# A two-layer streaming encoder on one core: a new order at both ends of its expert layers

## The chip, the cores and the metric

The kernel runs on one core of a Trainium2 chip. The metric is device time in microseconds of one execution. Before the change the median of three runs is 1529.91 us (1525.41 to 1532.59).

## What is computed

576 tokens of width 1024 (512 of a new stream, 64 of a running one) pass two layers. Layer 0 mixes tokens with an RG-LRU and an HGRN2 branch, layer 1 with an S5 state space and a gated output. After each mixer comes a normalization of alpha*x + f(x), then a mixture of 16 experts, then another normalization. Cut to what matters here:

```python
def _moe(x, router_w, router_b, w_gate, w_up, w_down):
    ...
    y = jnp.zeros(xt.shape, F32)
    for e in range(N_EXPERTS):
        h = jax.nn.silu(xt @ w_gate[e]) * (xt @ w_up[e])
        y = y + combine[:, e:e + 1] * (h @ w_down[e]).astype(F32)
    return y.reshape(Bn, T, D).astype(x.dtype)

def _post_norm(x, f, g, b):
    s = ALPHA * x.astype(F32) + f.astype(F32)
    mu = jnp.mean(s, -1, keepdims=True)
    var = jnp.mean(jnp.square(s - mu), -1, keepdims=True)
    return ((s - mu) * lax.rsqrt(var + LN_EPS) * g.astype(F32) + b.astype(F32)).astype(x.dtype)
```

Each token goes to two of the 16 experts. `w_gate` and `w_up` of an expert are 1024 x 512, `w_down` is 512 x 1024, all float32.

## The kernel before

The five engines run programs of their own (PE, ACT, DVE, POOL and SP) that wait on semaphores. A float32 product is made of three passes (`mm3`, lines 2276 to 2278): each operand is split into a rounded part "hi" and a remainder "lo". ACT makes hi by a copy that rounds, DVE makes lo by a subtraction, and PE adds hi*lo, lo*hi and hi*hi.

The tokens are first scattered by POOL to a buffer `xg` in memory, 96 rows (`CAP`) for each expert. For expert `it` the steps are:

- SP loads the three weight matrices, 2 MB each, into `raw[0]` (gate), `raw[1]` (up) and `raw[2]` (down), one buffer for each kind (line 547). A load waits until DVE has made the remainder of the matrix before it in this buffer (semaphores `lo0`, `lo1`, `lo2`).
- ACT rounds `raw[q]` to `whi[q]` (line 607), DVE subtracts to `wlo[q]` (line 685). Rounding waits for the load (`ld0` to `ld2`) and until PE has finished with the `whi[q]` of the expert before (`p_g`, `p_u`, `p_d`).
- PE transposes the expert's rows (`xt`, line 754), ACT and DVE split them (`xet_hi` line 613, `xet_lo` line 689).
- PE makes the gate product, up(0,it), and the up product, up(1,it), of 24 matmuls each (line 765). ACT takes Silu of the first (line 620), DVE multiplies it by the second (`h`, line 695).
- PE transposes that (`ht`, line 773), ACT and DVE split it (`ht_hi` line 626, `ht_lo` line 699), and PE makes the down product, down(it), of 24 matmuls (line 786).
- ACT evicts it to `ysb` (`y_ev`, line 632), and POOL stores it to `yg` (line 584). There is one `ysb`: an eviction waits for the store before it (`y_st`).

The order of each engine is written out by hand in the functions `step` of `experts_act`, `experts_dve` and `experts_pe`. PE runs up(0,it), ht(it-1), up(1,it), xt(it+1), down(it-1). The last expert has code of its own: its down weights are loaded in two halves, and each half is rounded, subtracted and multiplied by itself. Behind the experts POOL loads scale and bias of the normalization (`lng`, `lnb`, line 275), waits for the last store, and gathers each token's two rows from `yg` (line 839). DVE adds them to the residual and normalizes (lines 858 to 308). In layer 0, ACT and DVE split the first two halves of S5's input matrix (lines 1133 and 1300) before that.

Behind the 16 experts each engine reads a step count that the router has computed, and branches: tokens that found no place among the 96 rows of an expert would get further rounds of 16 steps.

## Time and profile before

| | |
|---|---|
| median of three runs | 1529.91 us (1525.41 to 1532.59) |
| the profiled execution | 1527.47 us |
| its span, first to last instruction | 1525.5 us |
| mean granted clock of PE | 0.872 of full speed |
| PE, DVE, ACT, POOL busy | 82%, 67%, 46%, 13% of the span |
| moved by DMA | 301.79 MB, 198 GB/s over the span |
| chain that ended last | PE 40%, DVE 24%, DMA 20%, ACT 9%, issue 5% |

The two expert layers lie at about 374 to 717 us (with the gathers' start) and 1140 to 1480 us of the span. Busy shares are means over stages with different limits, so the stages are looked at one by one. An engine's idle time before an instruction is given with what ended it. A "load" lands when its semaphore is raised.

### The profile page before, as it was taken

The numbers are of one execution on the slowest core, as the hardware profiler recorded it, in microseconds if no ns is written. First come the engines' busy times: TensorE is split into PE (matmuls) and PEld (weight loads), VectorE is DVE, ScalarE is ACT, GpSimd is POOL, SyncE is SP. The second block draws the span as 40 slices with busy tenths as digits, with TensorE's granted clock in tenths as the row PEclk, the third lists the DMA queues.
The fourth block names the chain that finished last, engine by engine and source line by source line (L and its number), as shares of the span: only waits on it lengthen the run. The fifth ranks groups of instructions, "written<-read, shape, count | busy, mean of one in ns | idle before, by whom it ended". The sixth has DMA issues, their size and how long they took to land.

```text
span 1525.5 us, 17350 instructions
## 1 busy us (share of the span) xinstructions
PE 1248.8 (82%) x6836; PEld 999.0 (65%) x6836; DVE 1021.9 (67%) x1039; ACT 701.5 (46%) x623; POOL 193.9 (13%) x219
## 2 busy tenths in 40 slices
PE   6999998796789999995694363999967899999950
PEld 5898888576667766763473253977756677776730
DVE  5883666346368888885867997343463688888828
ACT  4632333003367777774124243631332677777720
POOL 2020000000200000002203961000003000000021
PEclk9998997795699999997795676999966999999985
DMA  9455000412789999987453007351026899999845
GB/s 274 183 61 112 31 35 4 124 82 110 255 299 375 379 369 382 384 335 247 103 93 60 0 7 58 115 191 56 1 110 232 318 356 384 381 383 377 347 146 154
DMA packets 79568, 301.79 MB, mean 198 GB/s; under 512 B 23189, under 2 KB 40945, under 8 KB 66897
## 3 DMA queue, kind: packets, MB, share of 16 engines
q1 hardware_dynamic: 63416, 246.07, 47.4%
q0 software_dynamic: 16096, 54.96, 11.6%
q8 instruction: 38, 0.62, 0.2%
q14 instruction: 18, 0.14, 0.0%
HBM read 265.01 MB, written 33.64 MB: 196 GB/s over the span
## 4 chain that ended last, share of the span: by engine, by line
PE 40%; DVE 24%; DMA 20%; ACT 9%; issue 5%; SPq 1%; POOL 0%; POOLq 0%; ACTq 0%; DVEq 0%
PE ps L2276 9%; PE ps L2277 9%; PE ps L2278 9%; DVE wlo L685 7%; DMA raw<-in_moe_w_down 7%; DMA raw<-in_moe_w_gate 7%; ACT whi L607 6%; PE ps L746 3%; DMA u_d<-ub 2%; PE ps L1682 2%; PE ps L373 2%; DMA raw<-in_moe_w_up 1%; DMA raw<-in_w_in_ab 1%; DVE s_jtmp L1484 1%; PE ps L2386 1%
## 5 line engine op out<-in xcount | busy, mean ns | idle before, releaser
L685 DVE TENSOR_TENSOR wlo<-raw,whi 128x4096 fp32r<-128x4096 f32 x92 | 407.1, 4425 | 129.8 <-ACT whi L607 129.6
L607 ACT ACTIVATE whi<-raw 128x4096 fp32r<-128x4096 f32 x92 | 333.7, 3627 | 117.3 <-DMA raw<-in_moe_w_down 77.4
L2276 PE MATMUL ps<-whi,xet_lo 128*96 128x512 f32 x512 | 208.9, 408 | 28.4 <-ACT hx L620 24.3
L2277 PE MATMUL ps<-wlo,xet_hi 128*96 128x512 f32 x512 | 205.8, 402 | 0.0
L2278 PE MATMUL ps<-whi,xet_hi 128*96 128x512 f32 x512 | 205.8, 402 | 0.0
L2276 PEld LDWEIGHTS ps<-whi,xet_lo 128*96 128x96 f32 x512 | 86.3, 169 | 69.2 <-issue 35.7
L2276 PE MATMUL ps<-ft_hi,wlo 128*128 128x288 f32 x384 | 120.0, 312 | 5.1 <-DVE wlo L2023 3.6
L2277 PE MATMUL ps<-ft_lo,whi 128*128 128x288 f32 x384 | 116.9, 304 | 0.1
L2278 PE MATMUL ps<-ft_hi,whi 128*128 128x288 f32 x384 | 116.6, 304 | 0.0
L2276 PE MATMUL ps<-whi,ht_lo 128*96 128x512 f32 x256 | 104.1, 407 | 10.4 <-DVE ht_lo L699 8.7
L2278 PEld LDWEIGHTS ps<-whi,xet_hi 128*96 128x96 f32 x512 | 85.0, 166 | 37.1
L2277 PEld LDWEIGHTS ps<-wlo,xet_hi 128*96 128x96 f32 x512 | 85.2, 166 | 33.5 <-issue 0.5
L2276 PE MATMUL ps<-whi,ft_lo 128*120 128x512 f32 (+1 forms) x240 | 96.6, 403 | 11.8 <-DVE ft_lo L1308 6.1
L2278 PE MATMUL ps<-whi,ht_hi 128*96 128x512 f32 x256 | 102.2, 399 | 0.0
L2277 PE MATMUL ps<-wlo,ht_hi 128*96 128x512 f32 x256 | 102.1, 399 | 0.0
L2277 PE MATMUL ps<-wlo,ft_hi 128*120 128x512 f32 (+1 forms) x240 | 95.8, 399 | 0.0
L2278 PE MATMUL ps<-whi,ft_hi 128*120 128x512 f32 (+1 forms) x240 | 95.5, 398 | 0.0
L2276 PEld LDWEIGHTS ps<-ft_hi,wlo 128*128 128x128 f32 x384 | 76.2, 198 | 7.1 <-issue 6.3
L2277 PEld LDWEIGHTS ps<-ft_lo,whi 128*128 128x128 f32 x384 | 76.0, 198 | 0.5 <-issue 0.2
L2278 PEld LDWEIGHTS ps<-ft_hi,whi 128*128 128x128 f32 x384 | 75.6, 197 | 0.0
L584 POOL DMA_DIRECT2D yg<-ysb x32 | 16.2, 505 | 404.7 <-ACT ysb L632 404.7
L613 ACT ACTIVATE xet_hi<-ps 128x768 fp32r<-128x768 f32 x32 | 25.9, 809 | 83.5 <-PE ps L746 50.7
(449 smaller groups left out, 2234.9 us busy)
## 6 DMA issues: line engine op xcount, KB each, us to landing
raw<-in_moe_w_gate SPq DMA_DIRECT2D x32, 2048.0 KB, 9.9
raw<-in_moe_w_up SPq DMA_DIRECT2D x32, 2048.0 KB, 9.9
raw<-in_moe_w_down SPq DMA_DIRECT2D x30, 2048.0 KB, 10.2
yg<-ysb POOLq DMA_DIRECT2D x32, 384.0 KB, 6.0
xe<-xg POOLq DMA_DIRECT2D x30, 384.0 KB, 8.7
raw<-in_w_in_ab SPq DMA_DIRECT2D x16, 512.0 KB, 7.5
raw<-in_w_out_s SPq DMA_DIRECT2D x4, 2048.0 KB, 8.2
xg<-zeros POOLq DMA_DIRECT2D x4, 1536.0 KB, 14.5
```

The lines of the kernel that those rows point to most:

```text
L373: ins = te.matmul(ps[0:n, 6, E * i:E * i + E], x1t[:, k, 0:n], rw[:, k, :], start=(k == 0), stop=(k == KT - 1))
L584: pool.dma_start(rows, ysb[0:CAP, :]).then_inc(s("y_st" + L), 16)
L607: sa.activation(whi[q][:], raw[q][:], ACT.Copy).then_inc(s(f"hi{q}" + L), 1)
L613: sa.activation(xe_rows(xet_hi), xe_banks, ACT.Copy).then_inc(s("xth" + L), 1)
L685: v.tensor_tensor(wlo[q][:], raw[q][:], whi[q][:].bitcast(F32), ALU.subtract).then_inc(s(f"lo{q}" + L), 1)
L746: ins = te.matmul(ps[:, 4 + k // 4, P * (k % 4):P * (k % 4) + CAP], xtok[0:n, i, k:D:KT], onehot[0:n, i, :], start=(i == 0), stop=(i == NT ...
L1484: ins = tt(jtmp[:, k, 0:n], src, poles[lv][:, k, :, pairs].rearrange("p (x r) a -> p x r a", x=1).to_broadcast([P, n, 2, QP]), M)
L1682: ins = te.matmul(out, spad[(i // 2) % 2][:, ri, pair % QP, b, :], ox[:, ri, 1:CL + 1, pair, :], start=False, stop=(ri == 1))
L2276: te.matmul(out, l_lo, r_hi, start=first, stop=False)
L2277: te.matmul(out, l_hi, r_lo, start=False, stop=False)
L2278: return te.matmul(out, l_hi, r_hi, start=False, stop=last)
L2386: return te.matmul(out, vtok[rows, q // 2, :], sc[rows, q // 2, :], start=(q == 0), stop=True)
```

## The change

The start of a layer:

- ACT rounds and DVE subtracts the down weights of expert 0 before the tokens have arrived (`hi(2, 0)`, `lo(2, 0)`).
- In ACT's `step(it)`, Silu of expert `it` follows the split of the hidden rows of `it-1` and stands ahead of the rounding of the next gate weights. Before, it opened the step after.
- In DVE's `step(it)`, `h(it)` stands between the remainders of the next gate weights and the next tokens. Before, it opened the step after.

The end of a layer:

- The last down weights are loaded whole, into `raw[0]`, as soon as the remainder of the last gate weights is made, and split into `whi[0]` and `wlo[0]`.
- PE puts the transposes of the last hidden rows between the halves of down(14). Their split goes to `xet_hi` and `xet_lo`, and the last down product goes to the PSUM banks 0 and 1.
- In layer 0, the split of the first half of S5's input matrix (`s5_hi`, `s5_lo`, through `raw[1]`, now) stands ahead of the last eviction on ACT. The second half goes through `raw[0]`.
- POOL issues the loads of scale and bias ahead of the last store. The bias has a place of its own (`lnb_f`, over `ht_hi` and `ht_lo`), so its load waits for down(14).
- The wait for the last store moves into `gather`, behind the reading of the step count and the branch.

The core of the diff:

```diff
         def ln_gains_pool(pool, tag):
...
+            pool.dma_start(lng[:], a[f"ln_{ln}_g"][l:l + 1, :].to_broadcast([P, D])).then_inc(s("ln_gains"), 16)
+            if ln == "ffn":
+                pool.wait_ge(s(f"p_d_{l}"), E - 1)
+            pool.dma_start(lnb[:] if ln == "mix" else lnb_f[:], a[f"ln_{ln}_b"][l:l + 1, :].to_broadcast([P, D])
+                           ).then_inc(s("ln_gains"), 16)
...
         def experts_sp(sp_, l):
...
-            sp_.wait_ge(s("lo2" + L), E - 1)
-            for h_, name in enumerate(("ld2", "ld0")):
-                sp_.dma_start(raw[2][:, half * h_:half * h_ + half].rearrange("p (k n) -> p k n", k=2),
-                              w3[2][:, E - 1, 2 * h_:2 * h_ + 2]).then_inc(s(name + L), 16)
+            sp_.wait_ge(s("lo0" + L), E)
+            sp_.dma_start(raw[0][:].rearrange("p (k n) -> p k n", k=4), w3[2][:, E - 1]).then_inc(s("ld0" + L), 16)
...
         def experts_pool(pool, l):
...
-            for it in range(E - 3, E):
+            for it in range(E - 3, E - 1):
                 store_y(it)
+            pool.wait_ge(s("p_xt" + L), E)
+            ln_gains_pool(pool, f"ffn{l}")
+            store_y(E - 1)
...
-        def experts_act(act, l):
+        def experts_act(act, l, early=None):
...
-            def step(it, prev=True, prev2=True, nxt=True):
-                if prev:
-                    silu(it - 1)
+            def step(it, prev=True, prev2=True, nxt=True, down=True):
+                if prev and down:
                     hi(2, it - 1, "p_d")
                 if prev2:
                     y_ev(it - 2)
                 if prev:
                     ht_hi_(it - 1)
+                silu(it)
                 if nxt:
                     hi(0, it + 1, "p_g")
                     xt_hi(it + 1)
                     hi(1, it + 1, "p_u")

             hi(1, 0, "")
+            hi(2, 0, "")
             xt_hi(0)
             step(0, prev=False, prev2=False)
-            step(1, prev2=False)
+            step(1, prev2=False, down=False)
...
+            act.wait_ge(s("ld0" + L), 16 * E + 16)
+            act.wait_ge(s("p_g" + L), E)
+            for h_ in range(2):
                 half = slice(CHUNK // 2 * h_, CHUNK // 2 * h_ + CHUNK // 2)
...
+                sa.activation(whi[0][:, half], raw[0][:, half], ACT.Copy).then_inc(s("hi0" + L), 1)
+            act.wait_ge(s("p_ht" + L), E)
+            act.wait_ge(s("p_u" + L), E)
+            sa.activation(xet_hi[:, 0:4, 0:CAP], h_bank, ACT.Copy).then_inc(s("hth" + L), 1)
+            y_ev(E - 2)
+            if early:
+                early()
+            act.wait_ge(s("p_d" + L), E)
+            act.wait_ge(s("y_st" + L), 16 * E - 16)
+            sa.activation(ysb[0:CAP, :].rearrange("p (a c) -> p a c", a=2), ps[0:CAP, 0:2, :],
+                          ACT.Copy).then_inc(s("y_ev" + L), 1)
...
         def experts_dve(dve, l, early=None):
...
-            def step(it, prev=True, nxt=True):
+            def step(it, prev=True, nxt=True, down=True):
+                if prev and down:
+                    lo(2, it - 1)
                 if prev:
-                    h(it - 1)
-                    lo(2, it - 1)
                     ht_lo_(it - 1)
                 if nxt:
                     lo(0, it + 1)
+                    h(it)
                     xt_lo(it + 1)
                     lo(1, it + 1)
...
         def experts_pe(pe, mm3, l):
...
-            step(E - 1, nxt=False)
-            ht(E - 1)
+            up(0, E - 1, "p_g")
+            ht(E - 2)
+            up(1, E - 1, "p_u")
+            down(E - 2, between=E - 1)
...
         def combine_pool(pool, l):
             L = f"_{l}"
-            ln_gains_pool(pool, f"ffn{l}")
-            pool.wait_ge(s("y_st" + L), 16 * E)

             def gather(rows):
+                pool.wait_ge(s("y_st" + L), 16 * E)
                 for i, (t0, n) in enumerate(TILES):
...
         def s5_sp(sp_):
...
-            sp_.wait_ge(s("lo0_0"), E)
+            sp_.wait_ge(s("lo1_0"), E)
             load(0)
-            sp_.wait_ge(s("lo1_0"), E)
+            sp_.wait_ge(s("lo0_0"), E + 2)
             load(1)
...
-            experts_act(act, 0)
+            experts_act(act, 0, lambda: s5_hi(act, 0))
...
-            experts_dve(dve, 0)
+            experts_dve(dve, 0, lambda: s5_lo(dve, 0))
```

How the change moves instructions is shown at three places. Each row is an instruction with its line, what it writes and reads, and the semaphores it waits for. `whi_51` and `raw_49` are the buffers 0, `whi_52` and `raw_50` the buffers 1, `whi_164` (`whi_165` in the changed kernel) the buffer 2; `_0` at a semaphore's end is layer 0. The changed kernel's line numbers are higher by 1 to some 24.

ACT at the start of layer 0's experts, before:

```order
L607 ACTIVATE whi_52<-raw_50 128x4096 [waits ld1_0]
L613 ACTIVATE xet_hi<-ps 128x8x96 [waits p_xt_0]
L607 ACTIVATE whi_51<-raw_49 128x4096 [waits p_g_0,ld0_0]
L613 ACTIVATE xet_hi<-ps 128x8x96 [waits p_u_0,p_xt_0]
L607 ACTIVATE whi_52<-raw_50 128x4096 [waits p_u_0,ld1_0]
L620 ACT_TABLE_LOAD
L620 ACTIVATE hx<-ps 96x512 [waits p_g_0]
L607 ACTIVATE whi_164<-raw_163 128x4096 [waits ld2_0]
```

And in the changed kernel:

```order
L611 ACTIVATE whi_52<-raw_50 128x4096 [waits ld1_0]
L611 ACTIVATE whi_165<-raw_164 128x4096 [waits ld2_0]
L617 ACTIVATE xet_hi<-ps 128x8x96 [waits p_xt_0]
L624 ACT_TABLE_LOAD
L624 ACTIVATE hx<-ps 96x512 [waits p_g_0]
L611 ACTIVATE whi_51<-raw_49 128x4096 [waits p_g_0,ld0_0]
L617 ACTIVATE xet_hi<-ps 128x8x96 [waits p_u_0,p_xt_0]
L611 ACTIVATE whi_52<-raw_50 128x4096 [waits p_u_0,ld1_0]
```

The Silu (`hx`) with its table load has moved ahead of the rounding of the next gate weights, and the rounding of the first down weights ahead of the first tokens.

ACT at the end of layer 0's experts, before, from the split of expert 14's hidden rows:

```order
L626 ACTIVATE ht_hi<-ps 128x4x96 [waits p_d_0,p_ht_0]
L620 ACTIVATE hx<-ps 96x512 [waits p_ht_0,p_g_0]
L664 ACTIVATE whi_164<-raw_163 128x2048 [waits ld2_0,p_d_0]
L632 ACTIVATE ysb<-ps 96x1024 [waits y_st_0,p_d_0]
L626 ACTIVATE ht_hi<-ps 128x4x96 [waits p_d_0,p_ht_0]
L664 ACTIVATE whi_164<-raw_163 128x2048 [waits ld0_0]
L632 ACTIVATE ysb<-ps 96x1024 [waits y_st_0,p_d_0]
```

And in the changed kernel:

```order
L630 ACTIVATE ht_hi<-ps 128x4x96 [waits p_d_0,p_ht_0]
L624 ACTIVATE hx<-ps 96x512 [waits p_ht_0,p_g_0]
L668 ACTIVATE whi_51<-raw_49 128x2048 [waits p_g_0,ld0_0]
L668 ACTIVATE whi_51<-raw_49 128x2048
L671 ACTIVATE xet_hi<-ps 128x4x96 [waits p_u_0,p_ht_0]
L636 ACTIVATE ysb<-ps 96x1024 [waits y_st_0,p_d_0]
L1153 ACTIVATE whi_52<-raw_50 128x2048 [waits w_landed1]
L1153 ACTIVATE whi_52<-raw_50 128x2048
L677 ACTIVATE ysb<-ps 96x1024 [waits y_st_0,p_d_0]
```

The last down weights are rounded into buffer 0, waiting for the last gate product (`p_g`) and no longer for down(14) (`p_d`), and S5's first matrix half stands between the last two evictions.

POOL from the last stores to the first gather of layer 0, before, with the rows of the branch that is not taken left out of both pieces:

```order
L584 DMA yg<-ysb 96x1024 [waits y_ev_0] x3
L522 TENSOR_LOAD nstep [waits routed]
...
L275 DMA lng<-in_ln_ffn_g 128x1024
L275 DMA lnb<-in_ln_ffn_b 128x1024
L522 TENSOR_LOAD nstep [waits routed,y_st_0]
L522 ISA x2
L844 COMPARE_AND_BRANCH
L839 DMA ygat_167<-yg,slot 120x1024
```

And in the changed kernel:

```order
L585 DMA yg<-ysb 96x1024 [waits y_ev_0] x2
L276 DMA lng<-in_ln_ffn_g 128x1024 [waits p_xt_0]
L279 DMA lnb_f<-in_ln_ffn_b 128x1024 [waits p_d_0]
L585 DMA yg<-ysb 96x1024 [waits y_ev_0]
...
L527 TENSOR_LOAD nstep [waits routed]
L527 ISA x2
L863 COMPARE_AND_BRANCH
L858 DMA ygat_168<-yg,slot 120x1024 [waits y_st_0]
```

The two loads have moved ahead of the third store, and the wait for the store (`y_st`) from the second reading of the step count to the first gather.

## Rows read from the trace of the kernel before

**Rows 1.** Windows: us, then busy us (instructions) by engine, granted clock, DMA share, GB/s
```profile
412.00:470.00 58.00, 49.42 (x211) 35.07 (x212) 41.57 (x18) 42.28 (x22) 2.02 (x4) 0.91 0.85 310
470.00:510.00 40.00, 40.00 (x191) 29.05 (x190) 33.24 (x13) 28.55 (x17) 2.21 (x5) 1.00 1.00 392
...
677.00:700.00 23.00, 21.64 (x98) 15.15 (x96) 14.22 (x7) 11.09 (x7) 0.51 (x1) 1.00 0.61 229
```
**Rows 2.** Timeline of SP's queue: start us, us, engine, line, op; gate weights, experts 5, 15
```profile
475.45 0.33 SPq L547 DMA_DIRECT2D raw<-in_moe_w_gate  x1
...
660.81 0.33 SPq L547 DMA_DIRECT2D raw<-in_moe_w_gate  x1
```
**Rows 3.** Timeline of ACT, start of layer 0's experts; in brackets idle time before, what ended it
```profile
360.88 1.28 ACT L355 ACT_TABLE_LOAD   x1
364.67 0.27 ACT L355 ACTIVATE r_p<-r_w 120x80 f32<-120x80 f32 x1 [2.51 <-DVE r_w L423]
...
404.09 3.62 ACT L607 ACTIVATE whi<-raw 128x4096 fp32r<-128x4096 f32 x1 [9.49 <-PE ps L2278]
...
414.71 1.28 ACT L620 ACT_TABLE_LOAD   x1
416.00 0.59 ACT L620 ACTIVATE hx<-ps 96x512 f32<-96x512 f32 x1
```
**Rows 4.** Timeline of DVE, start of layer 0's experts
```profile
407.75 4.43 DVE L685 TENSOR_TENSOR wlo<-raw,whi 128x4096 fp32r<-128x4096 f32 x1 [12.16 <-ACT whi L607]
412.09 0.95 DVE L689 TENSOR_TENSOR xet_lo<-ps,xet_hi 128x768 fp32r<-128x768 f32 x1
```
**Rows 5.** Timeline of PE, first matmuls of the gate products of experts 1 and 2
```profile
416.74 0.71 PE L2276 MATMUL ps<-whi,xet_lo 128*96 128x512 f32 x1 [6.40 <-ACT hx L620]
...
441.00 0.44 PE L2276 MATMUL ps<-whi,xet_lo 128*96 128x512 f32 x1 [3.84 <-ACT hx L620]
```
**Rows 6.** DMA issues: the whole span's gate loads; then, 640 to 775, halves and stores
```profile
raw<-in_moe_w_gate SPq DMA_DIRECT2D x32, 2048.0 KB, 9.9
...
raw<-in_moe_w_down SPq DMA_DIRECT2D x2, 1024.0 KB, 6.5
yg<-ysb POOLq DMA_DIRECT2D x5, 384.0 KB, 5.7
```
**Rows 7.** Timeline of PE, last expert's matmuls: 1st and 13th of layer 0, 1st of layer 1
```profile
703.25 0.74 PE L2276 MATMUL ps<-whi,ht_lo 128*96 128x512 f32 x1 [4.35 <-DVE ht_lo L699]
...
708.47 0.39 PE L2276 MATMUL ps<-whi,ht_lo 128*96 128x512 f32 x1
...
1466.59 0.74 PE L2276 MATMUL ps<-whi,ht_lo 128*96 128x512 f32 x1 [4.35 <-DVE ht_lo L699]
```
**Rows 8.** Timeline of ACT, end of layer 0's experts
```profile
682.40 3.63 ACT L607 ACTIVATE whi<-raw 128x4096 fp32r<-128x4096 f32 x1 [1.33 <-DMA raw<-in_moe_w_down]
...
698.50 1.91 ACT L664 ACTIVATE whi<-raw 128x2048 fp32r<-128x2048 f32 x1 [10.00 <-PE ps L2278]
...
711.41 1.02 ACT L632 ACTIVATE ysb<-ps 96x1024 f32<-96x1024 f32 x1 [7.93 <-PE ps L2278]
```
**Rows 9.** Timeline of DVE, end of layer 0's experts
```profile
675.40 4.43 DVE L685 TENSOR_TENSOR wlo<-raw,whi 128x4096 fp32r<-128x4096 f32 x1 [0.26 <-ACT whi L607]
...
686.07 4.43 DVE L685 TENSOR_TENSOR wlo<-raw,whi 128x4096 fp32r<-128x4096 f32 x1 [0.43 <-ACT whi L607]
...
693.08 0.68 DVE L695 TENSOR_TENSOR hx<-hx,ps 96x512 f32<-96x512 f32 x1 [2.11 <-PE ps L2278]
```
**Rows 10.** Chain that ended last: start us, us, what; the last store of each layer
```profile
712.73 3.26 DMA yg<-ysb
...
1475.06 3.21 DMA yg<-ysb
```
**Rows 11.** Timeline of POOL, the first gather of each layer
```profile
717.59 2.10 POOL L839 DMA_INDIRECT ygat<-yg,slot  x1 [2.48 <-issue]
...
1480.21 1.02 POOL L839 DMA_INDIRECT ygat<-yg,slot  x1 [2.78 <-issue]
```

More of the change, by code:

```diff
@@ L532, in experts_sp, with load @@
                   a["moe_w_down"][l].rearrange("e (p k) n -> p e k n", p=P)]
-            half = CHUNK // 2
-            def load(q, e, it, further=0):
+            def load(q, e, it, done=0):
                 if isinstance(it, int) and it == 0:
@@ L711, in experts_dve @@
             lo(1, 0)
+            lo(2, 0)
             xt_lo(0)
             step(0, prev=False)
-            with dve.Fori(1, E - 1) as it:
+            step(1, down=False)
+            with dve.Fori(2, E - 1) as it:
                 step(it)
             step(E - 1, nxt=False)
-            h(E - 1)
             for h_ in range(2):
-                dve.wait_ge(s("hi2" + L), E + h_)
+                dve.wait_ge(s("hi0" + L), E + 1 + h_)
                 half = slice(CHUNK // 2 * h_, CHUNK // 2 * h_ + CHUNK // 2)
-                v.tensor_tensor(wlo[2][:, half], raw[2][:, half], whi[2][:, half].bitcast(F32),
-                                ALU.subtract).then_inc(s("lo2" + L), 1)
+                v.tensor_tensor(wlo[0][:, half], raw[0][:, half], whi[0][:, half].bitcast(F32),
+                                ALU.subtract).then_inc(s("lo0" + L), 1)
                 if h_ == 0:
-                    ht_lo_(E - 1)
+                    h(E - 1)
+            dve.wait_ge(s("hth" + L), E)
+            v.tensor_tensor(xet_lo[:, 0:4, 0:CAP], h_bank, xet_hi[:, 0:4, 0:CAP].bitcast(F32), ALU.subtract).then_inc(s("htl" + L), 1)
+            if early:
+                early()
             steps = step_count(dve, l)
@@ L755, in xt, with up @@
                 ins.then_inc(s("p_xt" + L), 1)
-            def up(q, it, done):
-                pe.wait_ge(s(f"lo{q}" + L), it + 1)
+            def up(q, it, done, more=0):
+                pe.wait_ge(s(f"lo{q}" + L), it + (1 + more))
                 pe.wait_ge(s("xtl" + L), it + 1)
@@ L774, in ht, with down @@
                 ins.then_inc(s("p_ht" + L), 1)
-            def down(it, further=0):
-                pe.wait_ge(s("lo2" + L), it + (1 + further))
+            def down(it, more=0, between=None):
+                pe.wait_ge(s("lo2" + L), it + (1 + more))
                 pe.wait_ge(s("htl" + L), it + 1)
@@ L787, in down @@
                                   k == 0, k == 3)
+                    if half == 0 and between is not None:
+                        ht(between)
                 ins.then_inc(s("p_d" + L), 1)
@@ L1291, in s5_act, with s5_lo @@
             x1t_copy(act, 1, NT - 2)
+        def s5_lo(dve, c):
+            tt, k = nc.vector.tensor_tensor, split_slot[c]
+            for h_ in range(2):
+                dve.wait_ge(s("hi_done"), s5_split(c, h_))
+                tt(wlo_s5[k][:, half_of(h_)], raw[raw_slot[c]][:, half_of(h_)], whi_s5[k][:, half_of(h_)].bitcast(F32),
+                   ALU.subtract).then_inc(s("lo_done"), 1)
         def s5_dve(dve, link, split_lo):
```

86 lines of the change are left out of this document (37 added, 49 removed).

## The prediction

> **What bounds the kernel now.** I read the windows first, then the waits at both ends of the expert layers, then the queues that feed them. In the windows [rows 1] the reader is to see three kinds of stretch. From 470 to 510 PE is busy for all of its 40.00 us, the clock is at 1.00 of full speed (2.4 GHz) and the DMA share is 1.00 at 392 GB/s: the loop over the experts is full on two resources at once. From 412 to 470, at the layer's start, PE has 49.42 busy of 58 us (8.6 idle), the clock averages 0.91 and DMA 0.85. From 677 to 700, at its end, DMA has dropped to 0.61. The SP queue [rows 2] gives the loop's pace: gate weights for expert 5 are requested at 475.45, for expert 15 at 660.81, so 18.54 us per expert. What a better order can win lies at the ends; inside, the same bytes must still move.
>
> **Start of a layer.** PE idles 6.40 us before up(0,1) and 3.84 us before up(0,2), both times ended by ACT's Silu [rows 5]. Silu of expert 0 had its product long before: ACT takes the rounding of gate(1) at 404.09 as soon as PE's gate product of expert 0 is done, then more work, then the table load at 414.71, and only at 416.00 the Silu [rows 3]. In the new order Silu stands ahead of that rounding. Its table load (1.28 us) can run while ACT waits for PE: an earlier table load at 360.88 ran ahead of an activation that then still waited 2.51 us for its input [rows 3]; ACT idled 9.49 us before 404.09, so I cost it at nothing. If that cover is gone, the price is 1.28 per layer.
> So Silu(0) runs 404.1 to 404.7, rounding gate(1) takes 3.62 to 408.3, DVE's remainder 4.43 to 412.8 (before: 407.75 + 4.43 = 412.2, so 0.6 later) [rows 3, 4]. Then DVE does h(0), now ahead of the token remainder: 0.68 [rows 9], then 0.95 [rows 4], to 414.5. PE starts up(0,1) there, not at 416.74: 2.2 us gained. At up(0,2) the Silu stood behind the scaling of the residual on ACT; now it is ahead of it, and the operands of expert 2 come from gate(2)'s load, whose request moved by +0.6 only. The down weights of expert 0 are rounded before the tokens arrive, while ACT and DVE wait (9.49 us and more), at no cost, and their buffer is then free for the next load at once, where before DVE freed it only after expert 1's other remainders. I count the whole 3.84 as gone: 6.0 together. With no stop, PE also keeps more of its clock; of the 0.09 that the mean granted clock lacks over 58 us (5.2 us of full-speed time, part of it in idle time) I take 0.8. **Start: 6.8 per layer.** Above, PE's idle time (8.6) and the DMA's free share (0.15 x 58 = 8.7) bound it at 8.6. Below, the bound is 0, if the loop gives it back.
>
> **The loop.** Silu (0.59) now precedes the rounding of the next gate weights on ACT, and h (0.68) precedes the token remainder and the up remainder on DVE. A load lands 9.9 us after its request in the loop, while the two halves of a down load at the layer's end land in 6.5 [rows 6]. The difference, some 3 us, is time spent queued behind other loads (an estimate from these two rows). A request that comes 0.6 to 1.3 us later only queues less. I cost the loop at 0.
>
> **End of a layer, layer 0.** PE waits 4.35 us for the last expert's hidden remainder and restarts at half speed: 12 matmuls take 703.25 to 708.47, 5.22 us, and the other 12 to the eviction at 711.41, 2.94 us [rows 7, 8]. The cause is that ACT may round the last down weights only when PE has released their buffer (the idle time of 10.00 before 698.50 ended by PE) [rows 8]. In the new order these weights land in buffer 0. They are requested after the gate remainder of expert 15, 675.40 + 4.43 = 679.8 [rows 9]. Queued behind the load that lands at 682.40 [rows 8], 2.10 MB at 392 GB/s take 5.35, so they land at 687.8. Two halves of 1.91 on ACT go to 691.6 [rows 8]. DVE finishes the down remainder of expert 14 at 686.07 + 4.43 = 690.5, then a half (2.2), h at 693.08 + 0.68 = 693.8 (up(1,15) ends it, as before), the other half to 696.0 [rows 9]. PE needs h in the middle of down(14), at about 695.5, and the halves when down(14) and the transposes end: 703.25 - 4.35 = 698.9. All are early by 1.7 us or more, so the 4.35 vanish and the restart too: 5.22 - 2.94 = 2.3. PE is done 6.65 earlier, at 704.8.
> Three things are added in front of the last eviction. ACT's two halves for S5's first matrix half (3.8) begin after the eviction of expert 14, at 700.0, and end at 703.8, before 704.8; if the matrix half landed after 701 it would hold the eviction. The eviction now also really waits for the store of expert 14: evicted 698.9 to 700.0, requested at 700.2, landing 5.7 later in this stretch [rows 6], 705.9. That costs 1.1. On POOL the two loads of scale and bias (1 MB) now stand ahead of the last store; their waits end with down(14), and POOL issues them before 702, so the instruction order costs nothing.
> The gathers now pass their branch first and then wait for the store. Before, the store lands at 712.73 + 3.26 = 715.99 [rows 10] and the first gather goes at 717.59 [rows 11]: 1.6 between them, filled by the reading of the step count and the branch; I take all of it. The Trainium skill (Advanced Engine Details and Errata, Control Flow Timing) puts a branch at 51 ns and a compare with branch at 108 ns. By that page alone little would be won by moving the wait, and the sum would stand at about 1502.5 instead. No row here prices the branch without the load of the step count.
> The DVE work on S5's matrix (before it ended shortly ahead of the first gathered rows) is earlier by about as much, so the gathers stay the last to arrive. **End of layer 0: 6.65 - 1.1 + 1.6 = 7.1.**
>
> **End of layer 1.** The last store is issued 8.47 after PE's restart (1466.59 to 1475.06), against 9.48 in layer 0, so the cold part is 1.0 shorter and PE's gain is 5.65. No S5 load competes; a store lands in 3.21 [rows 10], so the eviction does not wait for it. The gather follows its store's landing (1478.27) at 1480.21 [rows 11]: 1.9. **7.6.** The final normalizations follow unchanged.
>
> **Sum.** 2 x 6.8 + 7.1 + 7.6 = 28.3. The profiled execution took 1527.5 (span 1525.5 and 2.0 around it): **1499**. The median of the runs shown, 1529.9, stands 2.4 above that execution.
>
> **Rivals.**
> *The loop gives the start back (0.15).* If the loop is paced by something that the earlier start does not move, the first experts only queue longer, and 14.7 remains: 1512.8. For it: DMA is already at 1.00 by 470. Against: the bytes that did not move at 0.85 were lost time, and the total is the same.
> *The shared DMA engines delay the stores (0.07).* The scale and bias, 1 MB, move while the stores of experts 14 and 15 go out; at 392 GB/s they take 2.7. If each layer's last stores wait that long, layer 0 loses 2.7, layer 1 2.7 less the 1.1 of slack there: 1503.5. For it: a store's 5.7 near S5's loads against 3.21 alone [rows 6, 10]. Against: it is likely that most of that megabyte has moved by 705. The Trainium skill (DMA: Bandwidth & Descriptors, Issuing engines are not separate DMA queues) says that all issuers share the same 16 DMA engines, which speaks against putting these loads ahead of the store. The rows agree that neighbours stretch a store; no run here yet shows it for these loads.
> *The loop gets longer (0.05).* If not the DMA's rate but the ring of each buffer (load, round, remainder, next request) sets 18.54 us, then Silu and h lie on it: 0.59 + 0.68 = 1.27 in each of 13 turns in 2 layers, 33.0; the start's gain is lost too: 1527.5 - 14.7 + 33.0 = 1545.8, slower. It decides once a load's queueing time is under 1.27; the rows give some 3 [rows 6].
> *Nothing is won at either end (0.03)*, because a late landing holds ACT in front of the last eviction and the loop takes the start: 1527.
>
> **How the numbers follow.** The forecast has 0.70. The low end is both starts at 8.6 and no wait for the store, 1494.5, less some 3.5 for the spread of the runs (1525.4 to 1532.6): 1491. The high end holds the first rival and part of the second on top: 1516. About 0.5% (7.6 us) is what a measurement of this kernel can tell from no change. The forecast, the first two rivals and no more are faster by that: 0.91, of which I give 0.90; same 0.05, slower 0.05.
>
> **What would show it.** Right: PE's waits for Silu gone from both starts; the same 18.5 us between gate requests, shifted by 6 to 7; no PE idle time and a granted clock of 1.00 up to the last matmul of a layer; the first gather right behind its store's landing, 13 to 15 us earlier. Wrong: a pace above 19 us per expert; a wait of PE for h inside down(14); ACT waiting for S5's matrix ahead of the last eviction; the last eviction late behind a store.

## The result, and the profile after

The changed kernel takes **1507.02 us** (median of four runs, 1503.28 to 1510.12) where the kernel before takes 1531.06 (four runs, 1525.41 to 1532.59): a ratio of **0.984, interval 0.981 to 0.986**. The forecast was 1499 us, faster, with a range of 1491 to 1516. Two more comparisons, made beside the experiments below, gave 0.980 (0.978 to 0.982) and 0.984 (0.982 to 0.987).

The page of the changed kernel: span, busy time, and the chain that ended last.

```profile
span 1502.1 us, 17364 instructions
PE 1242.7 (83%) x6836; PEld 995.0 (66%) x6836; DVE 1019.8 (68%) x1039; ACT 701.2 (47%) x623; POOL 199.3 (13%) x219
PE 57%; DVE 20%; DMA 12%; ACT 5%; issue 4%; SPq 2%; POOL 0%; DVEq 0%; ACTq 0%; POOLq 0%
```

The span is 23.4 us shorter. PE has grown from 40% to 57% of the chain, DMA has gone from 20% to 12%. The windows, to be laid beside [rows 1] (the whole program lies 3.4 us later here when the experts of layer 0 begin):

```profile
412.00:470.00 58.00, 54.12 (x250) 38.92 (x249) 43.65 (x18) 41.37 (x23) 3.07 (x6) 0.97 0.89 340
470.00:510.00 40.00, 39.87 (x185) 28.28 (x184) 33.55 (x16) 29.79 (x15) 2.03 (x4) 1.00 1.00 384
...
677.00:700.00 23.00, 22.71 (x104) 16.20 (x103) 17.14 (x9) 14.24 (x10) 2.11 (x4) 1.00 0.81 296
```

At the start PE is busy for 54.1 of 58 us, not 49.4, and the granted clock is 0.97, not 0.91. At the end the DMA share is 0.81, not 0.61. The loop between is as full as it was, and its pace is 18.6 us per expert, against 18.54 in [rows 2] (gate weights of experts 5 and 15):

```profile
471.71 0.33 SPq L551 DMA_DIRECT2D raw<-in_moe_w_gate  x1
...
657.73 0.33 SPq L551 DMA_DIRECT2D raw<-in_moe_w_gate  x1
```

**The start.** ACT's timeline, beside [rows 3], and PE's, beside [rows 5]:

```profile
398.14 1.28 ACT L624 ACT_TABLE_LOAD   x1
407.44 0.60 ACT L624 ACTIVATE hx<-ps 96x512 f32<-96x512 f32 x1 [8.01 <-PE ps L2302]
407.93 3.62 ACT L611 ACTIVATE whi<-raw 128x4096 fp32r<-128x4096 f32 x1
```
```profile
417.57 0.45 PE L2300 MATMUL ps<-whi,xet_lo 128*96 128x512 f32 x1 [3.82 <-issue]
```

The table load runs while ACT waits for PE, so its cover held. Silu runs as soon as PE's product is done, and the rounding follows it at once. The wait of 6.40 us before up(0,1) is down to 3.82 us, and the one of 3.84 us before up(0,2) is gone: PE has no other wait up to 475.

**The end of layer 0.** ACT from the eviction of expert 14, and POOL up to the first gather:

```profile
695.25 1.02 ACT L636 ACTIVATE ysb<-ps 96x1024 f32<-96x1024 f32 x1 [2.26 <-PE ps L2302]
696.18 3.70 ACT L1153 ACTIVATE whi<-raw 128x2048 fp32r<-128x2048 f32 x2
702.63 1.02 ACT L677 ACTIVATE ysb<-ps 96x1024 f32<-96x1024 f32 x1 [2.74 <-DMA yg<-ysb]
```
```profile
696.57 0.51 POOL L585 DMA_DIRECT2D yg<-ysb  x1 [11.70 <-ACT ysb L636]
697.07 0.57 POOL L276 DMA_DIRECT2D lng<-in_ln_ffn_g  x1
697.62 0.56 POOL L279 DMA_DIRECT2D lnb_f<-in_ln_ffn_b  x1
703.94 0.53 POOL L585 DMA_DIRECT2D yg<-ysb  x1 [5.77 <-ACT ysb L677]
707.70 1.02 POOL L858 DMA_INDIRECT ygat<-yg,slot  x1 [3.23 <-DMA yg<-ysb]
```

PE has no idle time left between up(0,15), from 677.64 on, and the last matmul; the 4.35 us of [rows 7] and the restart are gone. The last eviction waits for the store of expert 14, as forecast. The first gather follows the landing of the last store (requested at 703.94, landed 3.46 later) by 0.3 us, where it was 1.6.

**By stretches.** The table cuts each profile at the same five events: POOL's first scatter of a layer, SP's requests for the gate weights of experts 5 and 15, DVE's first addition of gathered rows, and the end. Every number is the difference of two rows' start times, in us. "Ahead" is all before the first scatter, code that no kernel here changes. The stretch between the layers' experts (418.5 to 419.6) and the one behind the last addition (37.2 to 37.3) are alike in all kernels and left out.

| kernel | ahead | start 0 | loop 0 | end 0 | start 1 | loop 1 | end 1 | span |
|---|---|---|---|---|---|---|---|---|
| before | 379.5 | 96.0 | 185.4 | 65.7 | 95.3 | 184.4 | 63.6 | 1525.5 |
| changed, 1st | 382.9 | 88.8 | 186.0 | 57.9 | 89.2 | 185.3 | 56.3 | 1502.1 |
| changed, 2nd | 382.9 | 89.8 | 182.2 | 59.0 | 89.3 | 185.6 | 57.2 | 1502.4 |
| changed, 3rd | 385.6 | 89.5 | 188.5 | 59.8 | 87.7 | 187.3 | 57.5 | 1512.3 |
| start only | 387.8 | 88.8 | 185.6 | 65.0 | 89.4 | 186.2 | 64.2 | 1523.8 |
| order only | 386.0 | 87.7 | 182.2 | 65.0 | 88.8 | 187.9 | 63.2 | 1516.5 |
| end only | 381.0 | 96.2 | 186.9 | 60.0 | 95.6 | 187.0 | 57.0 | 1520.1 |
| wait back | 382.2 | 89.5 | 185.1 | 60.5 | 89.5 | 186.9 | 57.6 | 1507.4 |
| loads behind | 386.2 | 89.6 | 190.9 | 61.3 | 89.4 | 188.7 | 58.0 | 1520.2 |
| S5 behind | 385.8 | 89.4 | 186.4 | 59.4 | 88.0 | 186.1 | 56.9 | 1508.7 |
| S5 held | 388.8 | 88.5 | 186.3 | 71.2 | 87.4 | 184.1 | 57.3 | 1520.4 |
| two moves | 382.6 | 87.4 | 188.8 | 59.6 | 88.3 | 186.5 | 57.1 | 1506.9 |
| three moves | 382.1 | 87.7 | 185.1 | 58.2 | 86.4 | 185.7 | 56.9 | 1498.7 |
| loop twice | 387.7 | 90.3 | 190.4 | 60.7 | 90.3 | 187.3 | 57.9 | 1521.3 |

In the first pair (before, and changed 1st) the change is worth 7.2 and 6.1 us at the starts and 7.7 and 7.3 at the ends, the loops give back 0.7 and 0.9, and unchanged code ahead took 3.4 more: 23.4. Over the three profiles of the changed kernel the means are 89.4 and 88.7 at the starts and 58.9 and 57.0 at the ends, against 96.1 and 95.5 (two kernels with the old start) and 65.2 and 63.7 (three with the old end): 6.7 + 6.7 + 6.3 + 6.7 = **26.4 us**, which is also what the mean of the three ratios gives (1 - 0.983, times 1531: 26).

### The profile page after: what moved, and what is told of

Read it like the earlier page. It is cut to its first block, busy times and chain, and to the rows that moved or that the text cites. A ratio compares the mean times of both kernels' runs of the same rounds, so it can differ in the third digit from the quotient of the medians.

```text
span 1502.1 us, 17364 instructions
## 1 busy us (share of the span) xinstructions
PE 1242.7 (83%) x6836; PEld 995.0 (66%) x6836; DVE 1019.8 (68%) x1039; ACT 701.2 (47%) x623; POOL 199.3 (13%) x219
## 4 chain that ended last, share of the span: by engine, by line
PE 57%; DVE 20%; DMA 12%; ACT 5%; issue 4%; SPq 2%; POOL 0%; DVEq 0%; ACTq 0%; POOLq 0%
PE ps L2300 15%; PE ps L2302 14%; PE ps L2301 14%; DMA raw<-in_moe_w_down 7%; DVE wlo L695 4%; ACT whi L611 3%; PE ps L762 3%; DMA u_d<-ub 2%; PE ps L1706 2%; PE ps L378 2%; DVE s_jtmp L1508 1%; DMA raw<-in_w_in_ab 1%; PE ps L2410 1%; DVE s_wt L1465 1%; PE ps L1704 1%
## 5 line engine op out<-in xcount | busy, mean ns | idle before, releaser
L2300 PE MATMUL ps<-whi,xet_lo 128*96 128x512 f32 x528 | 213.5, 404 | 18.1 <-issue 13.6
L2302 PE MATMUL ps<-whi,xet_hi 128*96 128x512 f32 x528 | 210.6, 399 | 0.0
L2301 PE MATMUL ps<-wlo,xet_hi 128*96 128x512 f32 x528 | 210.3, 398 | 0.0
L2300 PE MATMUL ps<-whi,ht_lo 128*96 128x512 f32 x240 | 96.1, 401 | 1.6 <-DVE wlo L695 1.5
L2302 PE MATMUL ps<-whi,ft_hi 128*120 128x512 f32 (+1 forms) x240 | 95.6, 398 | 0.0
L2302 PE MATMUL ps<-whi,ht_hi 128*96 128x512 f32 x240 | 94.6, 394 | 0.0
L2301 PE MATMUL ps<-wlo,ht_hi 128*96 128x512 f32 x240 | 94.5, 394 | 0.0
L340 POOL DMA_INDIRECT xg<-xtok,slot x20 | 30.2, 1510 | 249.2 <-issue 248.9
```

What stands on the lines that cost most here:

```text
L340: pool.indirect_dma_start(out=xg, out_offset=bass.IndirectOffsetOnAxis(ap=slot[0:n, k, i:i + 1], axis=0), in_=xtok[0:n, i, :], in_offset=N ...
L2300: te.matmul(out, l_lo, r_hi, start=first, stop=False)
L2301: te.matmul(out, l_hi, r_lo, start=False, stop=False)
L2302: return te.matmul(out, l_hi, r_hi, start=False, stop=last)
```

## The experiments

Each kernel is compared with the kernel before on the same chip.

### Start only, order only, end only

The start alone is the kernel before with the start's lines of the diff; the order alone leaves out the early split of the down weights; the end alone is the changed kernel with the old lines there.

```diff
 start only, on ACT (DVE likewise with lo, h):
+            hi(2, 0, "")
...
-                if prev:
-                    silu(it - 1)
...
+                silu(it)
                 if nxt:
 order only, against the start only:
-            hi(2, 0, "")
-            lo(2, 0)
```

> The kernel before with the new order at the start of a layer alone. Theory of the forecast (the start's waits for Silu go, the loop keeps its pace of 18.5 us per expert): in the pair of profiles the start was worth 7.2 us in layer 0 and 6.1 in layer 1, so 13.3 us less than the kernel before, a ratio of 0.991; the request for the gate weights of expert 5 comes 6 to 7 us earlier, counted from the router's last stage, and PE's wait of 4.35 us before the last expert's down product stays. Rival, the loop gives the start back: ratio 1.000, the request for expert 15 not earlier at all. Rival, Silu and h lengthen the loop: about 33 us more in the loops, ratio 1.01.

> The changed kernel with the old order at the start of a layer: the end alone. Theory: the last gate request to the first gather is shorter by 6.8 us in layer 0 and 7.0 in layer 1, and the rows then arrive another 0.9 earlier, 14 to 15 us in all, a ratio of 0.990 to the kernel before; PE's waits of 6.40 and 3.84 us at the start are back, PE has no wait from up(0,15) to the last matmul. Rival (nothing is won at the end, since the last eviction waits for a landing): ratio 0.998 or more. If both parts are independent, this ratio times that of the start alone is the changed kernel's 0.984.

> The start of a layer alone, and of it only the places of Silu and h; the down weights of expert 0 are split where they were before. Theory of the forecast (both waits of PE are ended by a Silu that stands too late, so the order alone removes them): the stretch from the first scatter to the request for the gate weights of expert 5 takes 88.8 to 90.5 us in layer 0 (before 95.99, with the whole start 88.75) and 89.2 to 91 in layer 1 (before 95.29, with the whole start 89.44). Rival (the early split frees a buffer early, and the earlier load is what gains): 92 to 95 us in both.

Measured: start only 1522.56 us, ratio 0.993 (0.990 to 0.996); end only 1520.91, ratio 0.991 (0.988 to 0.994); order only 1520.66, ratio 0.991 (0.988 to 0.994). PE's first waits at the start, in the end-only kernel (two rows, columns as in [rows 5]) and in the order-only kernel (one row):

```profile
418.48 0.71 PE L2297 MATMUL ps<-whi,xet_lo 128*96 128x512 f32 x1 [6.40 <-ACT hx L624]
442.80 0.44 PE L2297 MATMUL ps<-whi,xet_lo 128*96 128x512 f32 x1 [3.84 <-ACT hx L624]
```
```profile
420.05 0.71 PE L2276 MATMUL ps<-whi,xet_lo 128*96 128x512 f32 x1 [3.82 <-issue]
```

And the start-only kernel has the old wait at the last expert:

```profile
704.66 0.74 PE L2279 MATMUL ps<-whi,ht_lo 128*96 128x512 f32 x1 [4.35 <-DVE ht_lo L699]
```

The two halves of the change are independent: each moves its own stretch and no other, and 0.993 times 0.991 is 0.984. The loop does not give the start back. And the order of Silu and h is all of the start's gain: with the down weights split in their old place the starts are 87.7 and 88.8 us, no longer than with the whole (88.8 and 89.4). The early split is worth nothing. Silu on ACT and h on DVE were moved together; what each is worth alone is not shown.

### Three parts of the end

POOL's wait for the last store ahead of the step count again ("wait back"); the loads of scale and bias behind the last store ("loads behind"); S5's first split behind the last eviction ("S5 behind").

```diff
 wait back, in combine_pool:
+            pool.wait_ge(s("y_st" + L), 16 * E)
             def gather(rows):
-                pool.wait_ge(s("y_st" + L), 16 * E)
 loads behind, in experts_pool:
+            store_y(E - 1)
             pool.wait_ge(s("p_xt" + L), E)
             ln_gains_pool(pool, f"ffn{l}")
-            store_y(E - 1)
 S5 behind:
-            experts_act(act, 0, lambda: s5_hi(act, 0))
+            experts_act(act, 0)
...
+            hi(0)
             hi(1)
```

> The changed kernel with POOL's wait for the last store ahead of the second reading of the step count, as before. Theory: reading the step count and the branch come back between landing and gather, where the kernel before had 1.6 us (layer 0) and 1.9 (layer 1) and the changed kernel has 0.3 and 0.66: the first gather comes 1.3 us later in each layer, 2.6 us more than the changed kernel. Rival, by the Trainium skill's 51 ns for a branch: under 0.3 us in both layers together. The distance from landing to gather in the trace tells them apart, the total is near what the runs can tell.

> The changed kernel with the loads of scale and bias behind the last store, as before. Rival of the forecast (these 1 MB share the DMA engines with the stores of experts 14 and 15 and delay them): the store of expert 14 lands in 3.3 to 4.5 us instead of 5.8, the last eviction of layer 0 comes up to 1.9 us earlier, layer 1's last store lands in 3.2 instead of 3.86; 2 to 3 us less than the changed kernel. Theory of the forecast (the 5.8 is S5's load of 2 MB, the loads of scale and bias matter little): landing of the store of expert 14 between 5.3 and 5.9, last eviction within 0.5 us of the changed kernel's, total within 1 us of it.

> The changed kernel with the split of S5's first matrix half behind the last eviction again, on ACT and DVE. Theory of the forecast (the gathered rows are the last to arrive, this split only fills idle time): the first row block is added (DVE) as long after the request for the gate weights of expert 15 as in the changed kernel, 57.9 to 59.0 us, and S5 is not longer; total unchanged. Rival, the early split is a part of the gain: DVE's four remainders of 2.2 us each then end about 716 us into the span, after the rows; 1 to 3 us more in this stretch.

**Wait back**: 1512.68 us, ratio 0.987 (0.984 to 0.991). POOL's last store and first gather of each layer:

```profile
703.21 0.53 POOL L585 DMA_DIRECT2D yg<-ysb  x1 [5.72 <-ACT ysb L677]
708.10 2.09 POOL L858 DMA_INDIRECT ygat<-yg,slot  x1 [4.36 <-issue]
...
1456.51 0.53 POOL L585 DMA_DIRECT2D yg<-ysb  x1 [3.88 <-ACT ysb L677]
1462.32 1.02 POOL L858 DMA_INDIRECT ygat<-yg,slot  x1 [5.29 <-issue]
```

From store to gather are 4.89 and 5.81 us; in the three profiles of the changed kernel 3.5 to 3.8 and 4.5 to 5.0. Part of this is the store itself. Its time to landing stands in the chain that ended last (start us, us), in this kernel and then in the changed one:

```profile
703.21 3.29 DMA yg<-ysb
...
1456.51 3.89 DMA yg<-ysb
```
```profile
703.94 3.46 DMA yg<-ysb
...
1452.72 3.86 DMA yg<-ysb
```

From landing to gather are 1.60 and 1.92 us here, as in the kernel before, and 0.30 and 0.66 in the changed kernel. So reading the step count and branching cost 1.3 us in each layer where they stand behind the landing. The total is later than the changed kernel's, by no more than the comparisons differ.

**Loads behind**: 1517.72 us, ratio 0.988 (0.985 to 0.992). In layer 0, against the rival, the store of expert 14 did not land sooner: the last eviction (ACT) waited 4.05 us for it, where it waited 2.53 to 3.80 in the three profiles of the changed kernel.

```profile
703.67 1.02 ACT L636 ACTIVATE ysb<-ps 96x1024 f32<-96x1024 f32 x1 [2.26 <-PE ps L2302]
...
712.34 1.02 ACT L677 ACTIVATE ysb<-ps 96x1024 f32<-96x1024 f32 x1 [4.05 <-DMA yg<-ysb]
```

But that wait goes with another load. The earlier the 2 MB of S5's second half are requested ahead of this store, the closer the last two evictions start: 4.09 us ahead 7.16 apart, 3.45 ahead 7.38, 3.40 ahead 8.44 (the three profiles of the changed kernel), 3.00 ahead 8.67 (here, requested at 701.98 and 704.98), 2.64 ahead 9.03 (end only). So layer 0 cannot tell what scale and bias do to that store. In layer 1, where no such load competes, the last store landed in 3.21 us, as the rival had it, and in 3.86 to 4.29 with the loads in front of it.

The first gather came as soon behind the store as in the changed kernel (3.76 and 4.04 us), but its rows took longer to arrive: 10.55 and 9.83 us from the first gather to the first addition, against 7.9 to 8.7 and 7.6 to 8.2. The same 1 MB now runs beside the gathers. End 0 is 61.3 us against the three profiles' 58.9, end 1 is 58.0 against 57.0. That the rows come later is clear. That the earlier place of these loads is a gain, of one to two us, is likely and not shown: this is one profile, and two other kernels with the changed end have nearly as much in layer 0 (end only 60.0, loop twice 60.7). The forecast had only the danger.

**S5 behind**: 1512.60 us, ratio 0.985 (0.981 to 0.988), beside 0.984 for the changed kernel in that comparison. End 0 is 59.4, inside the changed kernel's 57.9 to 59.8. DVE's split and its first addition:

```profile
711.08 8.90 DVE L1321 TENSOR_TENSOR wlo<-raw,whi 128x2048 fp32r<-128x2048 f32 x4 [12.96 <-ACT whi L1153]
720.96 1.28 DVE L877 SCALAR_TENSOR_TENSOR xtok<-ygat,gate,xtok 120x1024 f32<-120x1024 f32 x1 [0.98 <-DMA ygat<-yg,slot]
```

Even with all four remainders in a row DVE is done 0.98 us before the rows. The early split of S5's half is worth nothing here; it leaves DVE more idle time (5.63 us before 715.65 in the changed kernel).

### The last eviction's wait

"Two moves": the last eviction gets a buffer of its own, and in the first step alone the rounding of gate(1) and the token remainder go ahead of Silu and h. "S5 held": the changed kernel with the load of S5's second half behind the last store. "Three moves": two moves, and that load through `raw[2]`, early.

```diff
 two moves:
+        ysb_last = at("ysb_last", [P, D], FT_AT)
-            act.wait_ge(s("y_st" + L), 16 * E - 16)
-            sa.activation(ysb[0:CAP, :]...
+            sa.activation(ysb_last[0:CAP, :]...
 S5 held:
-            sp_.wait_ge(s("lo0_0"), E + 2)
+            sp_.wait_ge(s("y_st_0"), 16 * E)
             load(1)
 three moves:
-            sp_.wait_ge(s("lo0_0"), E + 2)
+            sp_.wait_ge(s("lo2_0"), E - 1)
             load(1)
```

> The changed kernel with two more moves. The last eviction goes to a buffer of its own (over the down weights, which are then done with), so it does not wait for the store of expert 14; in the first step alone, the rounding of gate(1) stands ahead of Silu(0) and the remainder of the tokens ahead of h(0). Theory: in layer 0 the last store follows the one before it after 5.5 us as in layer 1, not 7.37: 1.9 us less; the start is shorter by Silu and h, 0.5 + 0.68 us, in each layer: 87.6 and 88.0 us; 4.2 us less than the changed kernel in all. Rival (the wait for the store is only replaced by a later landing of the last store, and the start by another wait): no difference in either stretch.

> The changed kernel with the load of S5's second matrix half (2 MB) held until the last store of layer 0 has landed. Theory (this load is the neighbour that stretches the last two stores; what the DMA engines move first costs the other): the store of expert 14 lands in 3.3 to 4.5 us instead of 5.9, the last store is requested 5.5 to 6 us behind it instead of 7.37 and 7.16; the 2 MB then meet the gathers, rows come 2 to 5 us later than the landing says (from first gather to first addition 10 to 13 us instead of 8 to 8.7). Rival (the neighbours that matter are scale and bias): landing still 5.5 to 5.9.

> The version with two more moves, and a third: the second half of S5's matrix is loaded through the buffer of the down weights, which is free some 6 us earlier, while the DMA engines are idle (the places of gathered rows are exchanged so that the first go elsewhere). Theory: that load has then landed ahead of the last two stores; layer 0's last store is requested 5.5 us behind the one before it and lands in 3.3 to 3.6, against 11.1 us for both in the changed kernel and 11.65 in the version with two moves: 9.0 to 9.4; with the starts (87.4 and 88.3 us) some 4 us less than the changed kernel. Rival: scale and bias alone stretch the last store, 10.5 to 11.5 us for both, and no more is gained than at the starts, some 2 us.

> The changed kernel once more, beside the version with two more moves on the same chip. Its ratio to the kernel before should lie at 0.984 as in the first comparison, and its stretches within 1 us of those of its first profile (start 88.8 and 89.2, last store 7.37 behind the one before it in layer 0).

> The changed kernel a third time, beside these on the same chip: ratio between the 0.980 and 0.984 of the two comparisons so far.

**Two moves**: 1506.60 us, ratio 0.979 (0.977 to 0.982), beside 1506.02 and 0.980 for the changed kernel. ACT's last eviction, then POOL's last store and first gather:

```profile
701.84 1.02 ACT L681 ACTIVATE ysb_last<-ps 96x1024 f32<-96x1024 f32 x1 [0.98 <-PE ps L2309]
```
```profile
703.15 0.52 POOL L587 DMA_DIRECT2D yg<-ysb_last  x1 [4.00 <-ACT ysb_last L681]
709.20 2.22 POOL L865 DMA_INDIRECT ygat<-yg,slot  x1 [5.53 <-DMA yg<-ysb_last]
```

The eviction now waits only for PE, and the last store is requested 5.60 us behind the one before it, not 7.37. But it lands later: the gather goes 6.05 us behind it, not 3.76. The two together are 11.65, against 11.13, 10.63 and 11.93 in the three profiles of the changed kernel. On the store the rival was right: the wait moved from the eviction to the landing. At the start PE's wait before up(0,1) is shorter in layer 0, 3.09 us and not 3.82:

```profile
416.76 0.44 PE L2307 MATMUL ps<-whi,xet_lo 128*96 128x512 f32 x1 [3.09 <-DVE wlo L699]
```

The starts are 87.4 and 88.3 us. Among the kernels that have the changed kernel's start and loop, the first is shorter than any (88.5 to 89.8) and the second is not (87.4 to 89.5).

**S5 held**: 1521.91 us, ratio 0.989 (0.986 to 0.993). ACT's last two evictions and its next rounding:

```profile
701.15 1.02 ACT L636 ACTIVATE ysb<-ps 96x1024 f32<-96x1024 f32 x1 [2.26 <-PE ps L2302]
...
706.63 1.02 ACT L677 ACTIVATE ysb<-ps 96x1024 f32<-96x1024 f32 x1 [0.86 <-PE ps L2302]
728.44 3.71 ACT L1153 ACTIVATE whi<-raw 128x2048 fp32r<-128x2048 f32 x2 [20.79 <-DMA raw<-in_w_in_s]
```

With the 2 MB out of the way the store of expert 14 lands in time and the eviction waits for PE alone: S5's load is the neighbour that stretches that store. The price was far above what I expected: beside the gathers the load took some 16 us (requested behind the landing at about 712), DVE stands in line behind it, and end 0 grows to 71.2. DVE adds the first rows right behind that split, so when they arrived cannot be seen.

**Three moves**: 1508.06 us, ratio 0.982 (0.979 to 0.984), beside 1514.03 and 0.984 (0.982 to 0.987) for the changed kernel. The last store is requested 5.48 us behind the one before and the gather follows 4.43 later, 9.91 together: less than in the changed kernel, between what was expected (9.0 to 9.4) and its rival (10.5 to 11.5). But the rows then take 9.84 us, and end 0 is 58.2. Four orders of the same bytes (changed, two moves, three moves, S5 behind) all reach the first addition 57.9 to 59.8 us after the last gate request. The starts are 87.7 and 86.4 against 89.5 and 87.7. The medians favour this version by 6 us, but the intervals overlap: that it beats the changed kernel is not shown.

### The loop

Silu (ACT, shown) and the token remainder (DVE, likewise) are executed twice in each turn of the loop.

```diff
                 if twice:
+                    sa.activation(hx[0:CAP, :], ps[0:CAP, 0, :], ACT.Silu)...
                 sa.activation(hx[0:CAP, :], ps[0:CAP, 0, :], ACT.Silu)...
```

> The changed kernel with Silu executed twice on ACT (0.6 us more) and the remainder of the token rows twice on DVE (0.95 us more) in each of the 13 turns of the loop; the second result is the same as the first. Theory (the ring of load, rounding, remainder and next request has slack, a later request only queues less): the ten experts from the request for expert 5 to that for expert 15 take 185 to 187 us, as in the changed kernel (186.0 and 185.3). Rival, the ring sets the pace: 0.6 + 0.95 for each expert, 201 us per loop and 40 us in all.

Measured: 1528.69 us, ratio 0.997 (0.995 to 0.999), beside 1506.02 and 0.980 for the changed kernel: 22.7 us more, of 40 added. The profile is that of the lowest of its ten runs (1523.08) and shows only some 6 us in the two loops (190.4 + 187.3 against means of 185.6 + 186.0). Windows in the loop of layer 0, of the changed kernel and of this one (columns as in [rows 1]):

```profile
480.00:660.00 180.00, 176.00 (x815) 125.14 (x814) 147.76 (x60) 130.10 (x70) 10.14 (x20) 1.00 1.00 380
```
```profile
480.00:660.00 180.00, 172.95 (x792) 122.83 (x792) 151.91 (x66) 131.28 (x77) 9.61 (x19) 0.99 1.00 370
```

Neither theory holds for the total: only about half of the addition shows in the median. Where the 22.7 us lie is not shown. The two loops of this profile lie inside what the other thirteen profiles show without the addition (182.2 to 190.9), and so does the rate of 370 GB/s in the window (369 to 389 over their loops). The changed kernel's own order costs the loop nothing that can be seen: 184.4 to 187.0 us in the four loops with the old order, 182.2 to 188.5 in its six.

## Why the prediction was right, and where it was off

**Start, 6.8 per layer: right.** 7.2 and 6.1 in the first pair, 6.7 and 6.7 over all. The forecast left PE a wait of 4.2 us before up(0,1) (410.3 to 414.5); it is 3.82. The wait before up(0,2) went whole. The two waits make 6.4 us (forecast 6.0). In layer 0 that leaves 0.8 in the first pair and 0.3 over all for the clock, which the forecast put at 0.8; no run measures the clock's share alone. The early split was rightly costed at nothing; it also brings nothing.

**Loop, 0: right in size; the reason is weaker than it sounded.** "A later request only queues less" was put at some 3 us of slack, from loads that land in 9.9 and 6.5 us [rows 6]. But those loads differ in size, 2048 and 1024 KB: at the forecast's own 392 GB/s the second megabyte takes 2.7 of the 3.4 us, which leaves an estimate of 0.7 us of queueing, less than the 1.27 us that the forecast's own rival needs. By its own rule the forecast should then have leaned to the loop that gets longer. Added work of 1.55 us per turn does show, by 0.9 us per turn in the total. That this order costs the loop nothing is measured; the reason given for it is not shown, and the term came out right by luck.

**End, PE's part: right, by rows and not by a run of its own.** The request of the last store comes 5.7 us earlier in layer 0 (703.94 - 657.73 against 712.73 - 660.81; forecast 6.65 - 1.1 = 5.55) and 6.35 in layer 1 (1452.72 - 1408.63 against 1475.06 - 1424.62; forecast 5.65). The early load of the last down weights and the transposes between the halves of down(14) were not tried apart. The rows of layer 1, SP's request for expert 15 and POOL's last store and first gather:

```profile
1408.63 0.33 SPq L551 DMA_DIRECT2D raw<-in_moe_w_gate  x1
```
```profile
1452.72 0.53 POOL L585 DMA_DIRECT2D yg<-ysb  x1 [3.88 <-ACT ysb L677]
1457.24 1.02 POOL L858 DMA_INDIRECT ygat<-yg,slot  x1 [3.99 <-DMA yg<-ysb]
```

**The last eviction's wait, 1.1: the mechanism right, the size not.** Where no store is waited for, the last two evictions start 5.48 us apart (S5 held, 701.15 and 706.63); here it is 7.38, so the wait is 1.9 (7.16 and 8.44 in the other two profiles: 1.7 and 3.0). The store landed about as forecast; PE was done 5.5 us behind the eviction of expert 14, where I had put 5.9. In the two-moves kernel, taking this wait away won nothing: the next store landed that much later (5.75 us behind its request, not 3.46). With S5's load moved ahead as well (three moves) it landed in 4.13, so that load seems to have a part in it; what else has is open.

**Step count and branch, 1.6 and 1.9: mis-sized.** I took the whole distance from landing to gather. The wait-back kernel prices them at 1.3 in each layer; 0.3 and 0.66 us of the distance stay. From last store to first gather the change won 1.3 us in layer 0 (4.86 to a mean of 3.6), but only 0.4 in layer 1 (5.15 to 4.8), where the store now lands beside scale and bias, in 3.86 to 4.29 us and not 3.21 [rows 10]. The rule cited in the forecast (the Trainium skill, Advanced Engine Details and Errata, Control Flow Timing: 51 and 108 ns for a branch) would make the move worth almost nothing. The measurement decides: 1.3 us for the load of the step count and the branch together, some eight times the page's two figures added. No run has the branch alone.

**The sum.** The terms come to 28.3; the stretches measure 26.4: the starts 13.4 of 13.6, the ends 13.0 of 14.7, short mostly by the eviction's wait in layer 0 and the step count in layer 1. The step that failed most is the base: the sum was hung on one profiled execution of 1527.5, whose stretch ahead of the experts is the shortest of all fourteen profiles. Of the 7.9 us between 1499.2 (1527.5 - 28.3) and 1507.0, 3.6 are that execution's distance to the median of 1531.06; the other 4.3 are the effect, 24.0 in this comparison against 28.3. One sum of the forecast is off: its chances for the forecast and the first two rivals add up to 0.92, not 0.91, and nothing hangs on it.

**The rivals.** The loop does not give the start back (start only). The loop is not made longer by this order. The shared DMA engines do delay stores, through S5's load (S5 held) and, in layer 1, through scale and bias (from store to gather 4.04 us without them in front, 4.5 to 5.0 with them). The Trainium skill (DMA: Bandwidth & Descriptors, Issuing engines are not separate DMA queues) says that DMAs of all issuers run on the same 16 engines. The trace agrees: the eviction waits 2.74 us beside S5's load and 0.86 without it. But it does not follow that the loads are better behind the store: there they meet the gathers.

## What to carry to other kernels

Look for the one early instruction that stands behind work which must wait for something else (here a Silu whose product had long been done): the order of two instructions on ACT and DVE was half of this gain, and neither of the two early splits had a part in it. A wait that is taken away can come back at the next landing: four orders of the end reached the first addition within 1.9 us of one another. So measure between two fixed events before counting single waits. When two loads are compared for their queueing, compare loads of one size. Hang a forecast on the median, and on stretches that the change can touch, not on the span of one execution.

## What the hardware showed

**Scatters that stop for DVE.** In every kernel with the early split, POOL's second scatter takes 3.97 to 4.01 us where it took 1.01 to 1.04. The first two scatters and DVE's remainders at the start of layer 0, in the changed kernel:

```profile
382.90 3.38 POOL L340 DMA_INDIRECT xg<-xtok,slot  x1 [91.38 <-issue]
386.59 3.98 POOL L340 DMA_INDIRECT xg<-xtok,slot  x1 [0.30 <-issue]
```
```profile
380.92 8.75 DVE L695 TENSOR_TENSOR wlo<-raw,whi 128x4096 fp32r<-128x4096 f32 x2
```

and in the kernel before:

```profile
379.46 3.37 POOL L335 DMA_INDIRECT xg<-xtok,slot  x1 [91.40 <-issue]
383.14 1.01 POOL L335 DMA_INDIRECT xg<-xtok,slot  x1 [0.30 <-issue]
```
```profile
377.47 4.42 DVE L685 TENSOR_TENSOR wlo<-raw,whi 128x4096 fp32r<-128x4096 f32 x1
```

The first scatter ends 0.94 us behind the end of a remainder in both (385.34, half way through the pair, and 381.89), the second 0.90 us behind the end of the pair (389.67): each seems to begin only when a DVE instruction ends. A plain store does not stop: in the three-moves kernel one is issued in 0.52 us beside such a remainder.

```profile
698.82 0.52 POOL L587 DMA_DIRECT2D yg<-ysb_last  x1 [3.89 <-ACT ysb_last L681]
```
```profile
694.88 4.49 DVE L1330 TENSOR_TENSOR wlo<-raw,whi 128x2048 fp32r<-128x2048 f32 x2 [4.53 <-ACT whi L1163]
```

The Trainium skill (SBUF — State Buffer, Who interferes with whom) says that DVE and GpSimd share a port pair which is an exclusive lock, and that a DVE instruction with two SBUF inputs contends with a GpSimd instruction that reads SBUF. The rows agree, if it is the list of slots that is read. PE does not feel it: its first gate product begins 16.2 to 16.4 us behind the first scatter in both layers of every kernel, and its next wait is 3.82 us in layer 0 with and without the early split. The whole starts are 89.4 and 88.7 us against 87.7 and 88.8 in the order-only kernel, whose second scatter takes 1.01 and 1.04 us; from one profile of that kernel it is open whether the 1.7 in layer 0 is more than spread.

**What an unchanged stretch varies by.** The code ahead of the experts took 379.5 to 388.8 us. In the first pair the granted clock of one window differed (150 to 200 us; before, then changed):

```profile
150.00:200.00 50.00, 46.94 (x379) 44.48 (x379) 27.16 (x35) 15.51 (x20) 2.16 (x4) 0.95 0.13 47
```
```profile
150.00:200.00 50.00, 46.95 (x348) 44.32 (x347) 26.20 (x33) 14.06 (x17) 1.62 (x3) 0.84 0.14 48
```

The full loops vary too, from 182.2 to 190.9 us per ten experts. The DMA share is 0.99 to 1.01 in all of them, while the rate is 389 GB/s in the shortest and 369 in the longest: a full share does not mean one rate. So differences of 1 to 3 us, which is what most parts of this change are, are read from stretches and not from totals.
